# Expert rows of u and v stored side by side and gathered as pairs of 8 KB in the last stage of a two-block transformer kernel

## The chip, the cores and the metric

One NeuronCore of a Trainium2 chip runs the whole program. The metric is the device time in microseconds of one execution, lower is better. TensorE multiplies into PSUM, VectorE and ScalarE work elementwise and reduce, GpSimd issues most of the small and all of the indexed transfers here, SyncE issues the weight loads; 16 DMA engines carry all transfers.

## The reference

Two transformer blocks on 512 tokens of width 1024 in float32. The second block ends with a layer of retrieved experts (`_peer`), and the change is in that layer alone:

```python
def _peer(h, wq, k1, k2, u_tab, v_tab):
    ...
        q = (t @ wq).reshape(PEER_BLOCK, PEER_HEADS, 2, PEER_DQ // 2)
        ...
        v1, i1 = lax.top_k(s1, PEER_TOPK)
        v2, i2 = lax.top_k(s2, PEER_TOPK)
        cand = (v1[..., :, None] + v2[..., None, :]).reshape(...)
        score, ci = lax.top_k(cand, PEER_TOPK)
        expert = (... i1 ... * PEER_NKEYS + ... i2 ...)
        g = jax.nn.softmax(score, axis=-1).astype(t.dtype)
        act = jax.nn.gelu(jnp.einsum('thkd,td->thk', u_tab[expert], t))
        return jnp.einsum('thk,thkd->td', g * act, v_tab[expert]).astype(t.dtype)
```

Each token picks 8 heads x 16 = 128 of 16384 experts. For each it needs a row of u (1024 floats, 4 KB) for a dot product with the token, and the row of v with the same index for a weighted sum. That is 512 x 128 x 2 rows of 4 KB, 537 MB.

## The kernel before

Tokens lie in four tiles of 128, one token to a partition. One gather (`gather`, L2753) fetches for choice j of tile i the rows of all 128 tokens: 128 rows of 4 KB, 512 KB. There are 4 x 128 for u and as many for v, 1024 rows of work in the words of the kernel.

- `FETCH` is the order of gathers and of work: u rows, and behind them v rows, 16 of them within the 128 u rows of tile 0, then five v rows to four u rows, so that the v rows catch up with the u rows at the end.
- `PLACES` are buffers of 4 KB a partition: 7 until row 144, then 19. A gather waits until the row that had its place before was used: a dot for u, an add for v (`PREV`). All gathers stand on GpSimd's queue in the order of `FETCH`.
- For a u row VectorE makes the dot product (L2783). After every 16 of them (`BL`) it works out the polynomial of the gelu (L2788 to L2790), ScalarE the sigmoid (L2716), VectorE the weights (L2791, L2793).
- For a v row ScalarE makes a diagonal matrix of the weights (L2722, four buffers `DG`), and TensorE adds diagonal x row into PSUM (L2706, two matmuls of 512 columns, four records in the trace). An add is called by its row.
- The experts are chosen by `select_tensor` (scores, L2568), `select_scalar` (L2587 copies the scores, L2593 exponentiates) and `select_vector` (L2612 to L2663). One choice is that of one head in one tile: 32 in all. `EXU[i]` holds the indices.
- `in_order` weaves this on every engine: after each row of work the function `advance` lets the choices go on by two steps until row 128, then by two and one in turn, and the tail of the layer before (among it the queries of tiles 1 to 3, L258) by one step in three turns. If a gather needs indices that aren't there yet, `advance` runs until they are.
- At the end of a tile (v row 127) VectorE, ScalarE and GpSimd normalize and write the tile (L2806 to L2816, L2725, `to_power` at L263). `XHR` holds the rest of the sum; `LATE` are rows of constants.

## Time and profile before

| | us |
|---|---|
| median of 3 runs | 4134.59 |
| lowest, highest | 4134.58, 4135.83 |
| profiled execution | 4141.38 |
| its span, first to last instruction | 4139.6 |

Mean granted TensorE clock 0.936 of full speed. Busy shares of the span: TensorE 83%, VectorE 51%, ScalarE 22%, GpSimd 34%. The layer of experts with what is woven into it runs from 2463 us to the end. In the rows below PE is TensorE, PEld its weight load, DVE VectorE, ACT ScalarE, POOL GpSimd; a row of a timeline gives start, duration, engine, line, operation, count, and in brackets the idle time before it with what ended it.

### The profile page before, as it was taken

How to read it: one execution, taken by the hardware profiler on the slowest of the kernel's cores; microseconds unless marked ns; L12 is line 12 of the kernel's file. 1: busy time of each engine (PE TensorE's matmuls, PEld its weight loads, DVE VectorE, ACT ScalarE, POOL GpSimd, SP SyncE). 2: the span in 40 equal slices, each digit the busy share in tenths (PEclk: the TensorE clock that was granted, in tenths of full speed). 3: DMA queues.
4: the chain of work that ended last, by engine and by line, in shares of the span. 5: the costliest groups of instructions: out<-in, count | busy, mean ns of one | idle time of the engine just before them, and what ended most of it. 6: DMA issues, size and time to landing. Idle time of an engine off the chain costs nothing.

```text
span 4139.6 us, 32033 instructions
## 1 busy us (share of the span) xinstructions
PE 3437.5 (83%) x10366; PEld 1709.8 (41%) x10366; DVE 2123.9 (51%) x4564; ACT 906.0 (22%) x1862; POOL 1419.8 (34%) x1337
## 2 busy tenths in 40 slices
PE   8468998999998889988899974669776777788787
PEld 4344544444454454534444564234332323232222
DVE  0567424422004366757425449864686877444443
ACT  1224412000014123632211323111221222111111
POOL 0214410000000004700001013443777777777775
PEclk9768999999999999999999987789999899999999
DMA  3010021433221122211212356765999999999997
GB/s 143 21 51 1 1 102 51 162 134 151 102 82 41 66 87 69 93 67 56 92 61 81 130 189 216 260 233 189 350 380 356 332 378 376 380 409 409 367 408 314
DMA packets 171908, 764.63 MB, mean 185 GB/s; under 512 B 19256, under 2 KB 19256, under 8 KB 160224
## 3 DMA queue, kind: packets, MB, share of 16 engines
q0 software_dynamic: 157904, 580.06, 37.4%
q1 hardware_dynamic: 13824, 182.51, 12.0%
q8 instruction: 85, 1.39, 0.1%
q14 instruction: 79, 0.65, 0.0%
q10 hardware_dynamic: 16, 0.02, 0.0%
HBM read 743.62 MB, written 18.89 MB: 184 GB/s over the span
## 4 chain that ended last, share of the span: by engine, by line
PE 47%; DVE 16%; DMA 9%; POOL 9%; issue 6%; ACT 3%; POOLq 0%; DVEq 0%; ACTq 0%
PE ps L252 14%; PE ps L258 12%; POOL arena L2753 9%; DMA arena<-in_pu,arena 7%; DVE arena L2783 5%; PE ps L1346 5%; PE ps L1416 5%; DMA arena<-in_pv,arena 2%; PE ps L2706 2%; PE ps L220 2%; PE ps L1722 1%; PE ps L1710 1%; PE ps L2331 1%; PE ps L786 1%; PE ps L1031 1%
## 5 line engine op out<-in xcount | busy, mean ns | idle before, releaser
L2706 PE MATMUL ps<-arena 128*128 128x512 f32 x2048 | 999.4, 628 | 333.1 <-DMA arena<-in_pv,arena 169.5
L2783 DVE CUSTOM_DVE_ANT_0 arena<-arena 128x1024 f32<-128x1024 f32 x512 | 623.5, 1221 | 385.9 <-DMA arena<-in_pu,arena 385.2
L252 PE MATMUL ps<-arena 128*128 128x512 f32 (+1 forms) x1768 | 760.8, 591 | 31.2 <-ACT arena L2272 24.4
L2706 PEld LDWEIGHTS ps<-arena 128*128 128x128 f32 x2048 | 375.4, 196 | 936.1 <-issue 499.8
L2753 POOL DMA_INDIRECT arena<-in_pu,arena x512 | 546.1, 1067 | 373.2 <-DVE arena L2659 76.9
L2753 POOL DMA_INDIRECT arena<-in_pv,arena x512 | 548.4, 1071 | 196.1 <-issue 109.1
L258 PE MATMUL ps<-arena 128*128 128x512 f32 (+2 forms) x1408 | 532.4, 539 | 3.1 <-DVE arena L1263 0.9
L252 PEld LDWEIGHTS ps<-arena 128*128 128x128 f32 x1768 | 339.4, 193 | 438.5 <-issue 433.3
L258 PEld LDWEIGHTS ps<-arena 128*128 128x128 f32 x1408 | 268.8, 192 | 264.0 <-issue 218.6
L220 PE MATMUL ps<-arena 128*128 128x128 f32 x1046 | 192.9, 320 | 200.9 <-ACT arena L812 49.6
L2722 ACT ACTIVATE arena<-arena 128x128 f32<-128x128 f32 x512 | 191.6, 396 | 565.6 <-PE ps L2706 519.4
L1416 PE MATMUL ps<-arena 128*128 128x512 f32 x640 | 291.8, 607 | 24.7 <-ACT arena L1801 17.4
L263 POOL TENSOR_TENSOR arena<-arena 128x1 f32<-128x1 f32 (+7 forms) x38 | 61.3, 1615 | 687.7 <-DVE arena L630 291.8
L220 PEld LDWEIGHTS ps<-arena 128*128 128x128 f32 x1046 | 140.4, 162 | 286.4 <-issue 144.1
L1440 POOL DMA_DIRECT2D aside<-arena x20 | 10.7, 534 | 622.4 <-ACT arena L1430 622.4
L1346 PE MATMUL ps<-arena 128*128 128x512 f32 x512 | 221.5, 593 | 1.4 <-DVE arena L1380 1.4
L1416 PEld LDWEIGHTS ps<-arena 128*128 128x128 f32 x640 | 120.6, 195 | 161.5 <-issue 143.2
L1072 POOL TENSOR_SCALAR arena<-arena 128x128 f32<-128x128 f32 (+3 forms) x96 | 111.3, 1171 | 155.9 <-DVE arena L1103 87.7
L1246 POOL DMA_DIRECT2D x_spill<-arena x1 | 0.6, 573 | 464.3 <-DVE arena L1377 464.3
L1346 PEld LDWEIGHTS ps<-arena 128*128 128x128 f32 x512 | 96.7, 190 | 125.7 <-issue 123.4
L1554 DVE SCALAR_TENSOR_TENSOR ps<-arena,ps 128x512 f32<-128x512 f32 x150 | 113.4, 756 | 5.2
L1574 POOL TENSOR_TENSOR arena<-arena 128x512 f32<-128x512 f32 x90 | 105.4, 1171 | 24.3 <-ACT arena L1517 12.0
(342 smaller groups left out, 3218.1 us busy)
## 6 DMA issues: line engine op xcount, KB each, us to landing
arena<-in_w_in SPq DMA_DIRECT2D x27, 2048.0 KB, 9.0
arena<-in_w_ada SPq DMA_DIRECT2D x12, 2048.0 KB, 8.2
arena<-in_w_ff_in SPq DMA_DIRECT2D x8, 2048.0 KB, 12.7
arena<-in_w_ff_out SPq DMA_DIRECT2D x8, 2048.0 KB, 12.7
...
```

Source lines behind the costliest of these rows:

```text
L220: return t.transpose(ps, src, ID[0:src.shape[0], 0:src.shape[0]])
L252: x = t.matmul(PS[:, b, 0:n], hT[:, k, i * 128:(i + 1) * 128], w[:, k, :], start=k == 0, stop=k == nk - 1)
L258: x = t.matmul(PS[:, b, 0:n], w[:, k, f * 128:(f + 1) * 128], hT[:, k, 0:n], start=k == 0, stop=k == nk - 1)
L1072: g.tensor_scalar(probs(i, h), probs(i, h), r[:, 6 + h:7 + h], None, ALU.mult).then_inc(*at1.G.step("scaled", i, h))
L1346: x = t.matmul(PS[:, 4 * c + i, :], AT[:, 8 * kk + k, 128 * i:128 * i + 128], w[:, k, :], start=kk == 0 and k == 0, stop=kk == 3 and k == 7)
L1416: x = t.matmul(PS[:, b, :], l, r, start=k == 0, stop=k == 7)
L1554: tap.V.own(v).scalar_tensor_tensor(out=sums, in0=u[:, j:j + 512], scalar=tap_weight(k, j), in1=sums, op0=ALU.mult, op1=ALU.add).then_inc( ...
L1574: tap.G.own(g).tensor_tensor(cv, cv, TAPP[(30 * n + j - 1) % 3], ALU.add).then_inc(*tap.G.step("sum", 30 * n + j - 1))
L2706: x = t.matmul(PS[:, b + c, :], DG[n % 4], row(f)[:, 512 * c:512 * c + 512], start=j == 0, stop=j == 127)
L2722: a.activation(DG[n % 4], ID, ACT.Copy, scale=GS[i][:, j:j + 1]).then_inc(*pe.A.step("dg", n))
L2753: g.indirect_dma_start(PLACES[SPOT[n]], None, d[tab], bass.IndirectOffsetOnAxis(ap=EXU[i][:, j:j + 1], axis=0)).then_inc(s_row_in[SPOT[n]] ...
L2783: v.tensor_tensor_reduce(row(f), row(f), TT[i], 1.0, 0.0, ALU.mult, ALU.add, DOT[i % 2][:, j:j + 1]).then_inc(*pe.V.step("dot", 128 * i + j))
```

## The change

- The tables u and v are stored as one table `uv` of rows of 8 KB, u then v of the same expert (built with the weights on the host).
- Tile 0 works as before, with 7 places of 4 KB (`CELLS`) and rows of 4 KB: it reads `uv` as a table of half rows with twice the index, and `EXV` is the index of the v half. Its first 16 v rows stand where they stood; the other 112 now follow all u rows of the tile, ahead of tile 1.
- Tiles 1 to 3 gather u and v row together: 384 gathers of 128 x 8 KB, 1 MiB each, into 14 places (`PAIRS`), each held from the gather to the add. The v row of a choice is worked `LAG` = 6 choices behind its u row. Six of the places are the panels used before, eight are other pieces; some overlap the places of tile 0 (`SHARED`).
- In tiles 1 to 3 the gelu is worked in blocks of 4 instead of 16, and its polynomial takes two operations instead of three in all tiles.
- Some loads and operations of the end of a tile stand at other v rows (24 to 80, 96 to 112, 100 to 116), and `YY` and `XHR` lie elsewhere.

```diff
-        BL = 16
-        FETCH = []
+        BLOCK = (16, 4, 4, 4)
+        LAG = 6
+        UV = d["uv"]
+        HALVES = UV.rearrange("e (s n) -> (e s) n", s=2)
...
+        WORK = []
         done_v = 0
-        for n_ in range(1, 513):
-            FETCH.append(("pu", (n_ - 1) // 128, (n_ - 1) % 128))
-            goal = 0 if n_ < 64 else (n_ - 64) // 4 if n_ < 128 else 16 + (n_ - 128) * 5 // 4 if n_ < 512 else 512
...
+        for n_ in range(1, 129):
...
+            while done_v < (n_ - 64) // 4:
+                WORK.append(("pv", 0, done_v))
                 done_v += 1
-        ROWS = len(FETCH)
-        PLACES = [piece(o_cs + 1024), piece(o_ka + 1024), piece(o_ka + 2048), piece(o_cs), MIXf[:, 0:1024], piece(o_ht + 1024), piece(o_ka)]
-        FEW = len(PLACES)
-        PLACES += [panel("w_pq+", c)[:, 1024 * j:1024 * j + 1024] for c in (1, 2, 3) for j in range(4)]
-        MANY = len(PLACES)
-        FROM = 144
-        SPOT = [n % FEW if n < FROM else (n - FROM) % MANY for n in range(ROWS)]
...
+        WORK += [("pv", 0, j_) for j_ in range(done_v, 128)]
+        for n_ in range(384 + LAG):
+            if n_ < 384:
+                WORK.append(("pu", 1 + n_ // 128, n_ % 128))
+            if n_ >= LAG:
+                WORK.append(("pv", 1 + (n_ - LAG) // 128, (n_ - LAG) % 128))
...
+        CELLS = [piece(o_cs + 1024), piece(o_ka + 1024), piece(o_ka + 2048), piece(o_cs), MIXf[:, 0:1024], piece(o_ht + 1024), piece(o_ka)]
+        FEW = len(CELLS)
+        PAIRS = [panel("w_pq+", c)[:, 2048 * j:2048 * j + 2048] for c in (1, 2, 3) for j in range(2)]
+        PAIRS += [piece(o, 2048) for o in (o_va + 1024, o_ka + 2048, o_qa + 2048, o_ka, o_cs, W0, o_t + 2048, o_ht)]
+        MANY = len(PAIRS)
+        SHARED = {7: (2,), 9: (6, 1), 10: (3, 0), 11: (4,), 13: (5,)}
+        FETCH = [f for f in WORK if f[1] == 0]
+        SPOT = [n % FEW for n in range(256)]
+        FETCH += [("uv",) + f[1:] for f in WORK if f[1] and f[0] == "pu"]
+        SPOT += [FEW + n % MANY for n in range(384)]
...
+        for n_ in range(FETCHES):
+            k_ = SPOT[n_]
+            PREV.append([held_by[k_]] if uses[k_] else [held_by[c] for c in SHARED.get(k_ - FEW, ())])
+            uses[k_] += 1
+            NTH.append(uses[k_])
+            held_by[k_] = FETCH[n_]
...
+        def emptied(f):
+            return ("pu" if f[0] == "pu" else "pv",) + f[1:]
+        FREED = [max((WHEN[emptied(f)] for f in before), default=-1) for before in PREV]
...
         def row(f):
-            return PLACES[SPOT[NUMBER[f]]]
+            n = number(f)
+            if f[1] == 0:
+                return CELLS[SPOT[n]]
+            o = 1024 * (f[0] == "pv")
+            return PAIRS[SPOT[n] - FEW][:, o:o + 1024]
...
+        EXV = piece(o_ht + 2432, 128).bitcast(U32)
...
+                    if i == 0:
+                        pe.V.own(v).tensor_scalar(EXV[:, hs], EXU[0][:, hs], 1, None, ALU.add).then_inc(*pe.V.step("selv", h))
...
-                while n < ROWS and PREV[n] < r:
+                while n < FETCHES and FREED[n] < r:
...
-                yield FETCH[r]
+                yield WORK[r]
...
+                    bl = BLOCK[i]
+                    if tab == "pu" and j % bl == bl - 1:
+                        a.wait_ge(*pe.V.at("poly", i, j // bl))
+                        a.activation(T3[:, 0:bl], T3[:, 0:bl], ACT.Sigmoid, scale=2.0 * 0.7978845608028654
+                                     ).then_inc(*pe.A.step("gelu", i, j // bl))
...
+                if i == 0:
+                    g.wait_ge(*(pe.V.at("sel", 0, j // 16) if tab == "pu" else pe.V.at("selv", j // 16)))
+                    x = (EXU[0] if tab == "pu" else EXV)[:, j:j + 1]
+                    g.indirect_dma_start(CELLS[k], None, HALVES, bass.IndirectOffsetOnAxis(ap=x, axis=0)).then_inc(s_row_in[k], 16)
+                else:
+                    g.wait_ge(*pe.V.at("sel", i, j // 16))
+                    g.indirect_dma_start(PAIRS[k - FEW], None, UV, bass.IndirectOffsetOnAxis(ap=EXU[i][:, j:j + 1], axis=0)
+                                         ).then_inc(s_row_in[k], 16)
...
-                if f == ("pv", 0, 24):
+                if f == ("pv", 0, 80):
...
+                    bl = BLOCK[i]
+                    if j % bl == bl - 1:
+                        c = slice(j - bl + 1, j + 1)
+                        x, w, y = DOT[i % 2][:, c], GS[i][:, c], T3[:, 0:bl]
+                        pe.V.own(v).scalar_tensor_tensor(out=y, in0=x, scalar=0.044715, in1=x, op0=ALU.mult, op1=ALU.mult
+                                                         ).then_inc(*pe.V.step())
+                        pe.V.own(v).scalar_tensor_tensor(out=y, in0=y, scalar=1.0, in1=x, op0=ALU.add, op1=ALU.mult
+                                                         ).then_inc(*pe.V.step("poly", i, j // bl))
                         v.tensor_tensor(w, w, x, ALU.mult).then_inc(*pe.V.step())
-                        v.wait_ge(*pe.A.at("gelu", i, j // BL))
-                        pe.V.own(v).tensor_tensor(w, w, y, ALU.mult).then_inc(*pe.V.step("wg", i, j // BL))
```

What follows is the order of instructions in the two programs.

TensorE, tile 0, from the scores in the middle of it: L258 are the queries of tiles 1 to 3 (`x8` is one chunk), L2706 the adds of v rows, two to an add. Before:

```order
L2568 MATMUL ps<-arena 128x128 x4
L2706 MATMUL ps<-arena 128x512 x2
L258 MATMUL ps<-arena 128x384 x16
L2706 MATMUL ps<-arena 128x512 x2
L258 MATMUL ps<-arena 128x384 x40
L2706 MATMUL ps<-arena 128x512 x4
```

The same place now (L2597 is L2568, L2740 is L2706):

```order
L2597 MATMUL ps<-arena 128x128 x4
L2740 MATMUL ps<-arena 128x512 x2
L258 MATMUL ps<-arena 128x384 x16
L2740 MATMUL ps<-arena 128x512 x2
L258 MATMUL ps<-arena 128x384 x8
L2740 MATMUL ps<-arena 128x512 x2
L258 MATMUL ps<-arena 128x384 x8
L2740 MATMUL ps<-arena 128x512 x6
```

The five chunks that stood in one piece, and the five behind them with an add or two between, now have three adds between them, all of tile 0.

GpSimd, from the v rows of tile 0 to the first pairs of tile 1. Now (before, u and v gathers take turns here):

```order
L2800 DMA arena<-in_uv,arena 128x1024 x16
L2814 DMA arena<-in_rows 128x1024 x5
L2815 DMA arena<-ada_rows 128x1024
L2800 DMA arena<-in_uv,arena 128x1024 x41
L2803 DMA arena<-in_uv,arena 128x2048 x10
L263 TENSOR_TENSOR arena<-arena 128x1
```

Ten pairs are issued before GpSimd's part of the end of tile 0 (L263).

VectorE, tile 1, choices between dots (L2783 is a dot with its accumulator read). Before:

```order
L2783 ISA arena<-arena 128x1024
L2783 ISA arena 128x1
L2616 MATCH_REPLACE arena<-arena 128x128
L2618 MAX arena<-arena 128x8
L2620 MAX_INDEX arena<-arena 128x8
L2783 ISA arena<-arena 128x1024
L2783 ISA arena 128x1
L2612 MAX arena<-arena 128x8
```

The same kind of place now (L2833 is the dot, L2641 to L2697 are L2612 to L2663):

```order
L2833 ISA arena<-arena 128x1024
L2833 ISA arena 128x1
L2839 SCALAR_TENSOR_TENSOR arena<-arena 128x4
L2841 SCALAR_TENSOR_TENSOR arena<-arena 128x4
L2843 TENSOR_TENSOR arena<-arena 128x4
L2845 TENSOR_TENSOR arena<-arena 128x4
L2666 CAST arena<-arena 128x32
L2669 TENSOR_TENSOR arena<-arena 128x256
L2641 MAX arena<-arena 128x8
L2643 MAX_INDEX arena<-arena 128x8
```

Every fourth dot has the four operations of a gelu block behind it, and there are on average three steps of a choice between two dots. Of the choices, six are now done beside the v rows of tile 0, where no dots stand, and 17 beside the 161 dots behind them.

## Rows read from the trace of the kernel before

**Rows 1.** The page: GB/s in 40 slices of 103.5 us, and the packets.

```profile
GB/s 143 21 51 1 1 102 51 162 134 151 102 82 41 66 87 69 93 67 56 92 61 81 130 189 216 260 233 189 350 380 356 332 378 376 380 409 409 367 408 314
DMA packets 171908, 764.63 MB, mean 185 GB/s; under 512 B 19256, under 2 KB 19256, under 8 KB 160224
```

**Rows 2.** Windows of the expert stage: length, busy time by engine, clock, DMA share, GB/s.

```profile
core 0: us, PE busy (x) PEld busy (x) DVE busy (x) ACT busy (x) POOL busy (x), PEclk, DMA share, GB/s
2860.00:2880.00 20.00, 17.12 (x49) 8.59 (x48) 11.25 (x33) 2.86 (x8) 11.69 (x12) 1.00 0.72 253
3100.00:3500.00 400.00, 297.36 (x659) 120.60 (x658) 316.42 (x888) 81.29 (x210) 313.14 (x274) 0.94 0.97 360
3600.00:3700.00 100.00, 82.32 (x173) 29.97 (x173) 44.78 (x80) 16.83 (x45) 76.54 (x79) 1.00 1.03 409
```

**Rows 3.** A window at the program's start, while weights arrive in rows of 16 KB.

```profile
6.00:28.00 22.00, 13.44 (x48) 9.56 (x49) 5.91 (x9) 6.00 (x10) 1.02 (x1) 1.00 1.02 430
```

**Rows 4.** Timeline of GpSimd: gathers, among them number 600 and number 1000.

```profile
3104.35 1.96 POOL L2753 DMA_INDIRECT arena<-in_pv,arena  x1 [0.31 <-DVE arena L2614]
...
3551.51 0.94 POOL L2753 DMA_INDIRECT arena<-in_pu,arena  x1 [0.30 <-issue]
...
4079.74 1.00 POOL L2753 DMA_INDIRECT arena<-in_pv,arena  x1 [0.30 <-issue]
```

**Rows 5.** Timeline of TensorE in tile 0: scores, adds, and chunks of L258.

```profile
2816.03 1.13 PE L2568 MATMUL ps<-arena 128*128 128x128 f32 x8 [0.67 <-ACT arena L2378]
...
2833.24 1.96 PE L2706 MATMUL ps<-arena 128*128 128x512 f32 x4 [0.96 <-ACT arena L2722]
...
2883.42 5.34 PE L258 MATMUL ps<-arena 128*128 128x384 f32 x16
2889.72 3.67 PE L2706 MATMUL ps<-arena 128*128 128x512 f32 x8 [0.96 <-ACT arena L2722]
```

**Rows 6.** Timeline of the last tile's end: 18 adds, then VectorE's first and last operation.

```profile
4095.34 31.15 PE L2706 MATMUL ps<-arena 128*128 128x512 f32 x72 [1.82 <-ACT arena L2722]
...
4126.52 1.22 DVE L2806 TENSOR_TENSOR arena<-ps,arena 128x1024 f32<-128x1024 f32 x1 [31.41 <-PE ps L2706]
...
4134.69 1.23 DVE L2816 TENSOR_TENSOR arena<-arena 128x1024 f32<-128x1024 f32 x1
```

**Rows 7.** Timeline of VectorE: first and nearly last operation of one choice.

```profile
2452.83 0.30 DVE L2612 MAX8 arena<-arena 128x8 f32<-128x128 f32 x1 [1.17 <-ACT arena L2587]
...
2463.38 0.23 DVE L2659 TENSOR_SCALAR arena<-arena 128x16 f32<-128x16 f32 x1
```

**Rows 8.** Timeline of VectorE: a dot between two operations of a choice.

```profile
3213.14 0.42 DVE L2620 FIND_INDEX8 arena<-arena 128x8 uint32<-128x256 f32 x1
3213.48 1.21 DVE L2783 CUSTOM_DVE_ANT_0 arena<-arena 128x1024 f32<-128x1024 f32 x1
3214.61 0.08 DVE L2783 DVE_READ_ACCUMULATOR2_ANT arena<- 128x1 f32 x1
3214.73 0.17 DVE L2646 TENSOR_SCALAR arena<-arena 128x16 uint32<-128x16 uint32 x1
```

**Rows 9.** Timeline of VectorE: first and last operation of a gelu block.

```profile
4094.06 0.17 DVE L2788 TENSOR_TENSOR arena<-arena 128x16 f32<-128x16 f32 x1
...
4094.93 0.18 DVE L2793 TENSOR_TENSOR arena<-arena 128x16 f32<-128x16 f32 x1 [0.20 <-ACT arena L2716]
```

**Rows 10.** Groups of VectorE from 3220 to 3500 us that waited for ScalarE.

```profile
L2612 DVE MAX8 arena<-arena 128x8 f32<-128x128 f32 (+1 forms) x33 | 11.2, 341 | 12.3 <-ACT arena L2587 10.9
...
L2662 DVE RECIPROCAL arena<-arena 128x1 f32<-128x1 f32 x12 | 2.0, 164 | 3.4 <-ACT arena L2593 3.0
```

**Rows 11.** ScalarE's table load in a timeline, and one row of the DMA issues.

```profile
3135.71 1.28 ACT L2716 ACT_TABLE_LOAD   x1
...
arena<-in_ctx POOLq DMA_DIRECT2D x1, 1024.0 KB, 5.3
```

**Rows 12.** Timeline of TensorE: an add behind a gap.

```profile
2680.24 3.75 PE L2706 MATMUL ps<-arena 128*128 128x512 f32 x4 [5.04 <-ACT arena L2722]
```

88 lines of the change are left out of this document (44 added, 44 removed).

## The prediction

> **What bounds the kernel now.** I read the slices of the page first, then windows, then the timelines of GpSimd, TensorE and VectorE in the expert stage, which runs from 2463 us to the end. [rows 1] is the page's line of GB/s: from slice 29 on (about 2900 us) the core moves 350 to 410 GB/s, nowhere else as much. [rows 2] splits this. From 3600 to 3700 us the DMA engines are full (share 1.03, 409 GB/s), and GpSimd issues 79 gathers in 100 us; with the 0.30 us that stand before each of them, it is full too. From 3100 to 3500 us the rate is 360 GB/s: 274 gathers with 313.1 us of GpSimd plus 274 x 0.30 = 82 us, together 395 of 400. So there GpSimd's issue is the bound, as some gathers take 1.96 us instead of 0.94 [rows 4] while VectorE chooses experts. Around 2860 us neither is full (253 GB/s in that window, [rows 2]): TensorE works on the queries, in chunks of L258 [rows 5]. The chain of waits agrees: gathers, landings and dots take turns in it.
>
> Counting the gathers along GpSimd's timeline, number 144 (the first of tile 1) starts at 2836 us, number 600 at 3551.5 and number 1000 at 4079.7 [rows 4]: 1.32 us a row in the last part, two thirds of a tile end included, 2.64 us for a u and a v row.
>
> **Up to 2835 us nothing moves.** The TensorE order is the same up to the 15th add of tile 0, which starts at 2833.2 us [rows 5]. The smaller gelu of this stretch is unchanged (blocks of 16), its polynomial one operation of about 0.2 us shorter, and eight small operations for the v index are added: zero, under TensorE's work.
>
> **The middle: v rows of tile 0 alone.** In the new order the last 10 chunks of L258 stand with 26 adds of tile 0 (one chunk and 1 add, eight times a chunk and 3 adds, one chunk and 1 add), and the u rows of tile 1 that went beside them come later. A chunk is 5.34 us, the wait before the next add 0.96, two adds 3.67, a third 1.73 [rows 5, 6]: 8 x 11.5 + 2 x 8.1 = 108 us, to about 2943. 41 adds are then done. The other 87 have nothing beside them but three groups of scores (1.13 us and about 0.9 of waits each, [rows 5]): 87 x 1.73 (18 adds in 31.15 us, [rows 6]) = 150.5, + 6, + 2 for the late rows: TensorE ends tile 0 at 3102. Seven places are enough for that: a place comes round every 7 x 1.73 = 12 us, and a small gather lands in 5 to 6. The DMA engines run at 136 to 305 GB/s meanwhile; this is the loss of the change. Its cover is that 14 pairs are fetched from about 3090 on. Then VectorE ends the tile, 9.4 us from L2806 to L2816 [rows 6]; GpSimd gets to its part of it after ten pairs, 10 x 1.25 from 3090, just in time. The first dot on a pair starts at 3112.
>
> **The choice phase: VectorE becomes the bound.** Choices advance with the rows, three steps to two rows, before and after; so 17.3 heads are chosen beside the 161 dots that follow (before, one in 8.2 dots; now one in 9.3), and VectorE has for each: 161 dots x 1.17 (a dot pushes its neighbours 1.17 us apart, 3213.56 to 3214.73, [rows 8]) = 188; 17.3 heads x 11.2 (10.8 from the first MAX8 to L2659's end, the rest behind it, [rows 7]) = 194; 40 gelu blocks of four operations x 0.84 (a block of five operations takes 1.05, [rows 9]) = 34; the end of tile 1, 9.4 + 2; XHR 2.5. That is 430 us. Waits on ScalarE come on top: 10.9 + 3.0 us for 11 heads in 280 us now [rows 10], so 22; table loads of 1.28 us [rows 11] are twice as many, mostly done while ScalarE waits for VectorE anyway: 4, bounds 0 and 40. In all 456 us, 2.83 a pair: the DMA engines (2.48, below) and GpSimd (1.3 to 2.3 a pair) have slack. The phase ends at 3568.
>
> **The rest: DMA.** About eight pairs are then fetched ahead, 215 are not. What does a pair of 8 KB rows cost? The trace has no gathers of that size. From below: the weight loads of 16 KB rows at the start move 430 GB/s [rows 3], 2.44 us for 1 MiB. From above: twice a 4 KB gather at 409 GB/s, 2.56. I take a fixed part and a part by size through the two points: 160 ns for 4 KB and 610 for 16 KB on one engine give 310 for 8 KB, so 2.48 us a pair. 215 x 2.48 = 533; landing of the first 5.3 [rows 11]; the end of tile 2 keeps VectorE 12 us from dots, of which the 14 places cover all but 3. Last landing 3568 + 541 = 4109. The Trainium skill (DMA: Bandwidth & Descriptors, Why small descriptors are slow) gives a packet a fixed cost of about 3 cycles beside one for each 32 B; by that 8 KB rows would win 1.1% over 4 KB rows, an estimate of 2.53 us a pair and 11 us more in the sum. The two rows above differ by 5%, so I leave the sum as it is.
>
> **The tail.** ScalarE reaches the scale of v row j-6 behind the gelu of u row j, so with blocks of 4 seven adds, not four, come after the last dot: 1.3 + 0.4 + 0.25 + 0.5 to the first add, 7 x 1.73 + 0.2: 14.8. Now 18 adds and 32.5 us stand there [rows 6], but most of them beside the last v gathers. From TensorE's end to the end of the span 13.1, as now (4126.5 to 4139.6).
>
> **Sum.** 4109.5 + 14.8 + 13.1 = 4137.4, against the span of 4139.6: minus 2 us. The profiled execution is 6.8 us above the median of the runs, which I take as common to both: 4134.6 - 2 = **4132 us**. A gain of 33 us in the last part (215 pairs x 0.16) is eaten by the middle, where 112 rows go at TensorE's pace.
>
> **Rivals.**
> - *Faster: the waits of the choice phase vanish.* TensorE and ScalarE no longer wait for landings, six rows behind, so scores may be ready when VectorE asks: minus 22. With pairs at 430 GB/s another 215 x 0.04 = 9. Time 4101 to 4112. For it: nearly all of the 10.9 us come from adds that wait for landings. Against it: ScalarE is tied to VectorE at each block of four.
> - *Slower: TensorE is late for the scores.* With blocks of four it gets its adds in bursts of 7 us and then waits 4. After such a gap an add takes 3.75 us instead of 1.96 [rows 12]: the half clock, 1.2 GHz. Nine score groups then come 2 adds x 1.8 = 3.6 later, 32 in all, less the 6 that VectorE has to spare: plus 26, 4158. It decides from the point where the four adds of a block and the score group no longer end within the 11.4 us of four pairs. Where the granted clock stays near 1, it costs nothing.
> - *Slower: 8 KB rows are no faster by the byte than 4 KB rows.* 215 x 0.08 = 17: 4149; with the smaller win of 1%, 4143. For it: the start was loaded from another queue. The rule of the skill above speaks for this one.
> - *The change does not do what it says:* the descriptors of a row of 8 KB are made in two, GpSimd pays twice and stays at 2.86 us a pair: plus 60. Of 171908 packets 11684 are of 8 KB or more [rows 1], more than the some 10500 that the weight loads of 16 KB rows make (82 x 128), so GpSimd's direct loads of 8 KB rows are among them in one piece; this is unlikely.
>
> **How the numbers follow.** Forecast 0.42 (its own range 4120 to 4146, from the bounds of the middle, +-8, and of the table loads); waits vanish 0.25; late scores 0.17; no gain by row size 0.13; two descriptors 0.03. A measurement of this kernel tells 0.2%, 8.3 us, from no change: below 4126.3 is faster, above 4142.9 slower. Of the forecast 0.12 lie below, 0.24 between, 0.06 above; of the first rival 0.23 and 0.02; of the no-gain one 0.03 between and 0.10 above; the others above. Faster 0.35, same 0.29, slower 0.36. The range from 4104 to 4158 leaves out the far parts of the first two rivals and the last.
>
> **What would show it.** The last add of tile 0 near 3100 us, and about 300 GB/s or less from 2940 to 3090; VectorE over 90% busy from 3112 to near 3568, at 350 to 370 GB/s; behind that 420 to 425 GB/s with VectorE near 55%; a gather of a pair 1 to 2 us long on GpSimd; seven adds after the last dot. Wrong would be: tile 0 done before 3080 (the middle isn't TensorE's), VectorE with idle time in the choice phase (waits on ScalarE, or late pairs), or a rate in the last part of 409 or 430.

## The result and the profile after

| | before | after |
|---|---|---|
| median, us | 4134.59 | 4158.41 |
| lowest, highest (5 runs each) | 4132.02, 4139.55 | 4155.26, 4158.82 |
| profiled execution | 4141.38 | 4158.82 |
| its span | 4139.6 | 4157.0 |

The ratio of the times is 1.0061, with a 95% interval of 1.0049 to 1.0073: the change makes the kernel slower by 0.6%. Three later pairs of measurements gave 1.0058, 1.0067 and 1.0048. The predicted time was 4132 and its range 4104 to 4158, so the median lies 26 us above the one and 0.4 above the other.

The page's slices and packets of the changed kernel, the counterpart of [rows 1]:

```profile
GB/s 143 20 51 1 1 102 54 159 142 141 101 81 41 66 86 76 86 66 61 97 50 99 115 202 216 259 245 190 240 322 390 384 372 325 400 421 410 418 421 302
DMA packets 116610, 764.59 MB, mean 184 GB/s; under 512 B 13112, under 2 KB 13112, under 8 KB 55776
```

The packets fell from 171908 to 116610, as 384 gathers of 128 rows are in packets of 8 KB. Slice 28 (from 2910 us) moves 240 GB/s, and the slices behind 3600 us reach 421. The windows, to be held against [rows 2] (length; busy time of the engines; clock; DMA share; GB/s):

```profile
2860.00:2880.00 20.00, 18.08 (x48) 8.73 (x47) 10.24 (x40) 4.31 (x11) 5.68 (x6) 1.00 0.38 114
2950.00:3100.00 150.00, 143.04 (x341) 63.81 (x340) 50.00 (x177) 33.49 (x92) 82.59 (x89) 0.99 0.86 306
3100.00:3500.00 400.00, 285.05 (x588) 119.67 (x586) 336.90 (x995) 96.00 (x235) 158.39 (x143) 0.85 0.95 376
3600.00:3700.00 100.00, 78.94 (x156) 32.17 (x155) 54.03 (x119) 13.79 (x50) 44.51 (x40) 0.90 1.01 421
```

At 2860 us the rate has fallen from 253 GB/s to 114, from 3100 to 3500 it rose from 360 to 376, and from 3600 on from 409 to 421. GpSimd, which was full, now has 158 of 400 us and 45 of 100. So two stretches gained and one lost. How much, a count of the gathers says. It gives the rows of 4 KB that GpSimd had not yet asked for (a pair is two):

| at, us | before: rows left | after: rows left |
|---|---|---|
| 2835 | 880 | 879 |
| 2946 | 839 | 848 |
| 3116.6 | 718 | 742 |
| 3498 | 458 | 482 |
| 3570.9 | 408 | 434 |
| 4000 | 85 | 90 |
| last gather starts | 4108.9 | 4113.6 |
| end of the span | 4139.6 | 4157.0 |

In the middle, while tile 0 ends alone, the changed kernel falls 24 rows behind. In the choice phase it holds that distance and no more (two gained or lost). In the last part it makes good most of it: 434 rows in 542.7 us, 1.25 us each, where the kernel before needed 538 for 408, 1.32 each. The last gather is 4.7 us later; the other 12.7 of the 17.4 us come behind it, where a pair's landing and seven adds take the place of the last v rows' landings.

In the kernel before, GpSimd had no slack in the last part. Its waits ahead of its gathers from 3600 to 3700 us (total, times, longest) are all of 0.3 us or less, so it never stood waiting for a place:

```profile
POOL arena L2753 <- issue: 14.3, 47, 0.3
POOL arena L2753 <- PE ps L2706: 8.5, 28, 0.3
```

The 409 GB/s there are therefore as much the pace of GpSimd's issue as that of the DMA engines.

The end of tile 0 on VectorE and the first dots on pairs (start, duration, operation, wait in brackets):

```profile
3106.81 1.23 DVE L2858 TENSOR_TENSOR arena<-ps,arena 128x1024 f32<-128x1024 f32 x1 [12.37 <-PE ps L2740]
...
3114.99 1.23 DVE L2868 TENSOR_TENSOR arena<-arena 128x1024 f32<-128x1024 f32 x1
...
3116.59 1.22 DVE L2833 CUSTOM_DVE_ANT_0 arena<-arena 128x1024 f32<-128x1024 f32 x1
```

What VectorE waited for from there to dot number 160 (counted from 0), 3116 to 3571 us:

```profile
DVE arena L2641 <- ACT arena L2616: 19.1, 6, 4.0
DVE arena L2845 <- ACT arena L2751: 11.1, 39, 3.5
DVE arena L2696 <- ACT arena L2622: 6.4, 11, 1.2
DVE arena L2858 <- PE ps L2740: 2.7, 1, 2.7
```

Not one of them is a landing. Dot 160, the last choice's index and, from dot 168 on, the first dots that wait for a landing:

```profile
3570.87 1.22 DVE L2833 CUSTOM_DVE_ANT_0 arena<-arena 128x1024 f32<-128x1024 f32 x1
3572.01 0.08 DVE L2833 DVE_READ_ACCUMULATOR2_ANT arena<- 128x1 f32 x1
3572.12 0.18 DVE L2687 SCALAR_TENSOR_TENSOR arena<-arena 128x16 uint32<-128x16 f32 x1
...
3583.54 1.23 DVE L2833 CUSTOM_DVE_ANT_0 arena<-arena 128x1024 f32<-128x1024 f32 x1 [0.49 <-DMA arena<-in_uv,arena]
...
3587.57 1.23 DVE L2833 CUSTOM_DVE_ANT_0 arena<-arena 128x1024 f32<-128x1024 f32 x1 [2.79 <-DMA arena<-in_uv,arena]
```

The last dot and the end of the last tile, the counterpart of [rows 6]:

```profile
4128.87 1.23 DVE L2833 CUSTOM_DVE_ANT_0 arena<-arena 128x1024 f32<-128x1024 f32 x1 [1.19 <-DMA arena<-in_uv,arena]
...
4144.16 1.23 DVE L2858 TENSOR_TENSOR arena<-ps,arena 128x1024 f32<-128x1024 f32 x1 [13.22 <-PE ps L2740]
```

### The profile page after: what moved, and what is told of

Read it like the earlier page. It is cut to its first block, busy times and chain, and to the rows that moved or that the text cites. A ratio compares the mean times of both kernels' runs of the same rounds, so it can differ in the third digit from the quotient of the medians.

```text
span 4157.0 us, 31690 instructions
## 1 busy us (share of the span) xinstructions
PE 3463.3 (83%) x10366; PEld 1753.1 (42%) x10366; DVE 2152.1 (52%) x4828; ACT 910.3 (22%) x1946; POOL 1025.2 (25%) x953
## 2 busy tenths in 40 slices
DMA packets 116610, 764.59 MB, mean 184 GB/s; under 512 B 13112, under 2 KB 13112, under 8 KB 55776
## 4 chain that ended last, share of the span: by engine, by line
PE 51%; DVE 20%; DMA 10%; issue 4%; ACT 3%; POOL 2%; DVEq 0%; POOLq 0%; ACTq 0%
PE ps L252 14%; PE ps L258 12%; DMA arena<-in_uv,arena 10%; DVE arena L2833 7%; PE ps L2740 6%; PE ps L1346 5%; PE ps L1416 5%; PE ps L220 2%; POOL arena L2803 1%; PE ps L1722 1%; DVE arena L2643 1%; PE ps L1031 1%; DVE arena L2649 1%; DVE arena L2645 1%; PE ps L786 1%
## 5 line engine op out<-in xcount | busy, mean ns | idle before, releaser
L2740 PE MATMUL ps<-arena 128*128 128x512 f32 x2048 | 1020.0, 655 | 330.2 <-ACT arena L2758 307.2
L2740 PEld LDWEIGHTS ps<-arena 128*128 128x128 f32 x2048 | 416.0, 209 | 913.3 <-issue 855.9
L2833 DVE CUSTOM_DVE_ANT_0 arena<-arena 128x1024 f32<-128x1024 f32 x512 | 622.9, 1219 | 240.3 <-DMA arena<-in_uv,arena 240.1
L2803 POOL DMA_INDIRECT arena<-in_uv,arena x384 | 435.6, 1134 | 563.9 <-PE ps L2740 350.0
L258 PE MATMUL ps<-arena 128*128 128x512 f32 (+2 forms) x1408 | 532.3, 538 | 3.1 <-DVE arena L1263 0.9
L252 PEld LDWEIGHTS ps<-arena 128*128 128x128 f32 x1768 | 339.3, 193 | 437.6 <-issue 432.5
L258 PEld LDWEIGHTS ps<-arena 128*128 128x128 f32 x1408 | 268.3, 191 | 263.8 <-issue 219.5
L2800 POOL DMA_INDIRECT arena<-in_uv,arena x256 | 265.1, 1035 | 385.4 <-PE ps L2740 144.7
L1416 PE MATMUL ps<-arena 128*128 128x512 f32 x640 | 291.6, 606 | 24.7 <-ACT arena L1801 17.4
L220 PEld LDWEIGHTS ps<-arena 128*128 128x128 f32 x1046 | 141.0, 162 | 284.6 <-issue 146.6
L263 POOL TENSOR_TENSOR arena<-arena 128x1 f32<-128x1 f32 (+7 forms) x38 | 61.2, 1613 | 715.8 <-DVE arena L630 291.5
L1346 PE MATMUL ps<-arena 128*128 128x512 f32 x512 | 221.5, 593 | 1.4 <-DVE arena L1380 1.4
L2758 ACT ACTIVATE arena<-arena 128x128 f32<-128x128 f32 x512 | 173.1, 389 | 123.7 <-PE ps L2740 110.2
L2751 ACT ACTIVATE arena<-arena 128x4 f32<-128x4 f32 (+1 forms) x104 | 21.5, 207 | 806.5 <-DVE arena L2841 806.4
L1416 PEld LDWEIGHTS ps<-arena 128*128 128x128 f32 x640 | 120.5, 195 | 161.4 <-issue 143.1
L1346 PEld LDWEIGHTS ps<-arena 128*128 128x128 f32 x512 | 96.7, 190 | 125.7 <-issue 123.4
## 6 DMA issues: line engine op xcount, KB each, us to landing
arena<-in_w_ff_out SPq DMA_DIRECT2D x8, 2048.0 KB, 12.7
```

Source lines behind the costliest of these rows:

```text
L220: return t.transpose(ps, src, ID[0:src.shape[0], 0:src.shape[0]])
L252: x = t.matmul(PS[:, b, 0:n], hT[:, k, i * 128:(i + 1) * 128], w[:, k, :], start=k == 0, stop=k == nk - 1)
L258: x = t.matmul(PS[:, b, 0:n], w[:, k, f * 128:(f + 1) * 128], hT[:, k, 0:n], start=k == 0, stop=k == nk - 1)
L1346: x = t.matmul(PS[:, 4 * c + i, :], AT[:, 8 * kk + k, 128 * i:128 * i + 128], w[:, k, :], start=kk == 0 and k == 0, stop=kk == 3 and k == 7)
L1416: x = t.matmul(PS[:, b, :], l, r, start=k == 0, stop=k == 7)
L2740: x = t.matmul(PS[:, b + c, :], DG[n % 4], row(f)[:, 512 * c:512 * c + 512], start=j == 0, stop=j == 127)
```

## The experiments

The times are medians; "changed" is the changed kernel. It was measured four times, each beside a kernel before of 4130 to 4135 on the same chip: 4158.4, 4154.9, 4158.8 and 4155.6 us. On two further occasions the kernel before took 4219 and 4231 us, and there the changed kernel did not run; where a version ran on one of those the text says so, and its distance from the changed kernel is then one between occasions. From the traces (all in us of the span; dots on pairs are counted from 0):

| kernel | first dot | dot 160 | last dot | span | median |
|---|---|---|---|---|---|
| changed | 3116.6 | 3570.9 | 4128.9 | 4157.0 | 4158.4 |
| slower choices | 3114.7 | 3516.2 | 4080.2 | 4107.6 | 4110.5 |
| two gathers a pair | 3129.2 | 3605.8 | 4198.0 | 4227.1 | 4226.7 |
| distance 4 | 3115.5 | 3568.7 | 4120.3 | 4144.3 | 4147.6 |
| distance 8 | 3111.8 | 3560.1 | 4123.4 | 4154.2 | 4156.9 |
| gelu blocks of 2 | 3116.7 | 3604.5 | 4162.7 | 4190.1 | 4191.8 |
| mixed middle | 2954.4 | 3531.1 | 4087.6 | 4115.0 | 4115.7 |
| slower choices, distance 4 | 3117.7 | 3517.7 | 4080.2 | 4104.1 | 4105.7 |
| these and mixed | 2948.9 | 3495.5 | 4057.0 | 4080.9 | 4083.1 |
| these, tile ends apart | 2947.6 | 3488.3 | 4049.4 | 4073.3 | 4075.4 |
| these, a fifth place | 2951.2 | 3484.6 | 4046.6 | 4070.6 | 4072.6 |

### Slower choices

```diff
-                drain(chosen, 2 if r < 128 or turns[0] % 2 else 1)
+                drain(chosen, 1 if r >= 256 else 2 if r < 128 or turns[0] % 2 else 1)
```

> The changed kernel with one edit: from row 256 of the order on (the first pair), a choice advances one step a row (two a pair) instead of three steps to two rows. No work is left out. Theory A, VectorE bounds the choice phase: VectorE's work for a pair falls to 1.17 (dot) + 0.21 (a quarter of a gelu block) + 2 steps x 0.40 (11.2 us for 28 steps of a choice) = 2.2 us, with the waits on ScalarE 2.35, under the 2.49 that a pair takes in the DMA-bound part. The pairs then go at 2.49 to 2.52 us from the first dot at 3116 on: last dot 3116 + 383 x 2.51 = 4077, median about 4107, 52 us below the changed kernel and 27 below the kernel before. VectorE is never over 95% busy behind 3116, the last choice ends near 3750. Theory B, the choice phase is slow because TensorE gets its adds in bursts at half clock and frees places late: bursts are the same, the phase goes on at 2.8 a pair and lasts until the last choice: 4160 to 4190.

It took 4110.49 us (4106.45 to 4111.99), beside a kernel before of 4231. The window from the first dot to 3700 us, and VectorE's waits in it:

```profile
3115.00:3700.00 585.00, 446.18 (x968) 186.72 (x969) 489.96 (x1379) 133.91 (x365) 260.84 (x230) 0.92 1.00 415
```

```profile
DVE arena L2833 <- DMA arena<-in_uv,arena: 35.7, 74, 2.5
DVE arena L2641 <- ACT arena L2616: 15.6, 7, 3.4
DVE arena L2845 <- ACT arena L2751: 12.0, 57, 0.9
```

The dots now wait for landings already while experts are chosen, and the DMA engines' share is 1.00. The 160 pairs from the first dot took 401.5 us, 2.51 each, where the changed kernel took 2.84. Theory A's 4107 is met within 4 us; theory B, which had the phase go on at 2.8, is refuted. The last choice now ends at 3713 us instead of 3572. The same bytes and the same VectorE work in another proportion are worth some 48 us.

### Two gathers a pair

Each pair comes in two gathers of 4 KB rows, from tables of u and of v; who waits for a pair waits for both.

```diff
-                    g.indirect_dma_start(PAIRS[k - FEW], None, UV, bass.IndirectOffsetOnAxis(ap=EXU[i][:, j:j + 1], axis=0)
-                                         ).then_inc(s_row_in[k], 16)
+                    for half, tab_ in enumerate(("pu", "pv")):
+                        g.indirect_dma_start(PAIRS[k - FEW][:, 1024 * half:1024 * half + 1024], None, d[tab_],
+                                             bass.IndirectOffsetOnAxis(ap=EXU[i][:, j:j + 1], axis=0)).then_inc(s_row_in[k], 16)
```

> The changed kernel with one edit: each pair is fetched by two gathers of 4 KB rows, u and v, into the same place, from two tables of their own; order, places, gelu blocks as changed. It measures what 8 KB rows are worth by themselves. If a 4 KB gather takes 1.28 us of the DMA engines (409 GB/s) and a pair 2.487 (422 GB/s), the 222 pairs behind 3571 us take 2.56 each: plus 16 us, 4174. If the row size is worth nothing: 4158. If GpSimd's issue comes in (two gathers of 0.94 to 1.96 us and 0.30 before each, 2.5 to 4.5 a pair, 2.9 as in the kernel before while VectorE chooses): the 161 pairs of the choice phase take 2.9 instead of 2.83 as well, plus 11: 4185.

4274.35 us (4269.45 to 4282.26), on the occasion on which the kernel before took 4231. As that left the size open, it ran once more beside the changed kernel.

> The kernel with two 4 KB gathers a pair once more, beside the changed kernel and the kernel before on one chip. On the chip of the first call it took 4274 us, at 365 to 375 GB/s behind 3600 us with the DMA engines' share at 0.97 to 0.99, but the kernel before took 4231 there, 97 more than elsewhere, and has as many 4 KB gathers. If that chip (or where its tables lay) was slow with 4 KB gathers alone: here 409 GB/s behind 3600 us, 2.56 a pair, and 4170 to 4180. If a pair in two gathers is slow everywhere (GpSimd's issue with 0.30 before each): 4260 to 4275 here too, with the kernel before at 4134.

Here it took 4226.68 us (4209.82 to 4228.98) beside 4158.82 for the changed kernel and 4129.71 for the one before: 68 us above the changed kernel. So no expectation held: row size alone was priced at 4174, with GpSimd's issue at 4185. The traces part the 70.1 us between the spans: the first dot is 12.6 later, the 160 pairs behind it take 22.3 more, the rest 34.2 more, the tail 1. In the choice phase (3150 to 3450 us) and behind it (3620 to 3720):

```profile
3150.00:3450.00 300.00, 215.07 (x459) 90.84 (x458) 249.11 (x756) 70.81 (x180) 239.05 (x202) 0.90 0.95 348
3620.00:3720.00 100.00, 73.72 (x151) 30.02 (x149) 51.31 (x114) 12.77 (x47) 77.49 (x75) 0.91 1.01 392
```

and GpSimd's gathers in the first of these windows (count, busy us, mean ns, idle before them):

```profile
L2804 POOL DMA_INDIRECT arena<-in_pv,arena x100 | 123.3, 1233 | 30.5 <-issue 23.5 <-DVE arena L2846 1.2 <-DVE arena L2649 1.2
L2804 POOL DMA_INDIRECT arena<-in_pu,arena x101 | 116.3, 1152 | 34.7 <-issue 18.0 <-PE ps L2740 5.4 <-DVE arena L2645 1.5
```

239.6 us of gathers and 65 before them are the whole of 300: GpSimd is the bound at 348 GB/s, as it was in the kernel before. From 3620 to 3720 us it is full as well, 77.5 us and 0.3 before each of 74 gathers, and none of them waited longer:

```profile
POOL arena L2804 <- issue: 19.8, 65, 0.3
POOL arena L2804 <- PE ps L2740: 1.8, 6, 0.3
```

The 56.5 us of both parts go with the number of issues. What the row size does to the DMA engines by itself this run does not tell, as they were not the only bound in either window; a DMA share of 1.01 at 392 GB/s, and of 1.01 at 421 with pairs, says that the share doesn't either. Why the first dot is 12.6 us later was not followed up. Put together, by the medians taken side by side: order, places, distance and gelu blocks of the change cost 97 us (4129.7 to 4226.7), and the pair gathers give 68 back.

### The distance from dot to add

```diff
-        LAG = 6
+        LAG = 4
```

> The changed kernel with one edit: the add of a pair's v row stands 4 rows behind its dot, not 6. A place then comes free two pairs earlier, so two more of the 14 are in flight or landed. Theory A (at the end of the choice phase there was no stock of landed pairs because 6 to 9 of the 14 places wait for their add): the stock at the hand-over is 2 pairs larger, minus 5 us; the adds behind the last dot are five, not seven, minus 3.5: 4150. If the missing stock has another cause: 4155, by the tail alone. If the shorter distance lets TensorE or ScalarE hold up VectorE (ScalarE is tied to it at each block of four): above 4158.

4147.63 us (4146.10 to 4158.67), on the occasion on which the kernel before took 4231. And with `LAG = 8`:

> The changed kernel with one edit: the add of a pair stands 8 rows behind its dot, not 6. Theory A (places are held until their add, and that is why no stock of landed pairs stood at the end of the choice phase): 8 to 11 of the 14 places wait for their add, 3 to 6 are in flight, and a landing takes 13.7 us, so also the choice phase waits for landings and the DMA engines idle in the last part: at 4.5 pairs in flight per some 12.5 us 2.8 us a pair, 222 x 0.3 = 67 us more at worst, at the least 5 for the stock and 3.5 for the two more adds at the end: 4170 to 4225, 4190 as the middle. Rival, places don't matter: 4162.

4156.92 us (4155.48 to 4167.21), beside 4154.94 for the changed kernel. The expected 4190 was wrong. What VectorE waited for from 3570 to 3620 us with 4, and with 8:

```profile
DVE arena L2833 <- DMA arena<-in_uv,arena: 15.7, 15, 1.3
```

```profile
DVE arena L2833 <- DMA arena<-in_uv,arena: 21.4, 21, 1.3
```

In the last part all three move 421 GB/s. In the steady state 9, 7 and 5 pairs were issued and not yet dotted with distances of 4, 6 and 8. One of them has landed, so with 8 some four are in flight (3.9 on average from 3620 to 3720 us, 3 to 5), and these are enough to keep the DMA engines full: a pair then just spends less time in the queue, as the times from issue to landing show (minimum, median, maximum; with 8 for all 384 pair gathers, with 4 for the 54 whose landing the trace has; it was 13.7 in the median with 6):

```profile
DMA to landing us min/median/max: 5.5/10.1/20.8
```

```profile
DMA to landing us min/median/max: 5.7/18.0/23.8
```

What the distance does move is the stock at the end of the choice phase, the pairs that have landed and are not yet dotted. The first dot that waits for a landing behind dot 160 is number 170 with a distance of 4, 168 with 6, 165 with 8, and the 20 pairs from dot 160 on take 1.94, 2.20 and 2.35 us each. Against 2.487 that is a stock of 4.4, 2.3 and 1.1 pairs. The landings themselves, counted at the start of dot 160, give three pairs ahead with a distance of 6 and one with 8. The tail from the last dot to the end is 24.0, 28.1 and 30.8 us. Both together are the 7 to 11 us that the distance of 4 gains; with 8 the part from dot 160 to the last dot is 5.3 us longer and the tail 2.7, but in the profiled execution its first dot was 4.8 us earlier and its choice phase 6.0 shorter (448.3 us), so no loss is left. Why, was not followed up.

### Gelu blocks of two

```diff
-        BLOCK = (16, 4, 4, 4)
+        BLOCK = (16, 2, 2, 2)
```

> The changed kernel with gelu blocks of 2 instead of 4 for tiles 1 to 3. VectorE then has 80 blocks of 0.84 instead of 40 in the choice phase, ScalarE twice the sigmoids, TensorE bursts of two adds with half the gap. Theory A (the choice phase is VectorE's work): plus 40 x 0.84 = 34 in 161 pairs, 3.04 a pair, nothing behind it as VectorE has slack there, and one or two adds less at the end: 4185. Theory B (bursts of adds at the half clock make scores late and frees places late): the waits of 27 us on ScalarE's copies and exponentials shrink to 10, and the end of the block's add comes earlier: 4158 + 34 - 17 = 4175 if the blocks cost VectorE in full, less if their waits are hidden; a time under 4160 would say that bursts cost more than I think.

4191.84 us (4188.15 to 4197.27), on the occasion on which the kernel before took 4219. VectorE's waits from 3110 to 3600 us:

```profile
DVE arena L2845 <- ACT arena L2751: 22.7, 79, 3.5
DVE arena L2641 <- ACT arena L2616: 13.9, 5, 5.0
DVE arena L2696 <- ACT arena L2622: 8.4, 11, 1.2
```

First dot to dot 160: 487.8 us against 454.3, so 33.5 more, where theory A had 34. VectorE was busy 22.2 us longer (413.0 against 390.8), and the waits for sigmoids grew by 11.6. The waits for scores and exponentials (L2641, L2696) are 22.3 us, hardly less than the 25.5 of the changed kernel, although the adds come in twos. So their size does not hang on the size of the bursts, as theory B had it, and every operation on VectorE, with its waits for sigmoids, counts in this phase in full. What the half clock by itself costs there this run does not tell: with gaps between the adds still there, the granted clock from 3100 to 3600 us was 0.89.

### The mixed middle

From v row 44 of tile 0 on, one pair of tile 1 stands beside each v row. The places are dealt out anew for it, the four diagonals go round by the order of the adds, and the load of `XHR` for tile 1 moves from v row 64 to 104.

```diff
+        ALONE = 44
...
-        WORK += [("pv", 0, j_) for j_ in range(done_v, 128)]
+        WORK += [("pv", 0, j_) for j_ in range(done_v, ALONE)]
+        done_v = ALONE
         for n_ in range(384 + LAG):
+            if done_v < 128:
+                WORK.append(("pv", 0, done_v))
+                done_v += 1
```

> The changed kernel with one edit of the order: from v row 44 of tile 0 on, each v row stands with a pair of tile 1 (with the places that this needs). Distance 6, pace of the choices and tile ends as in the changed kernel. Slower choices with the distance of 4, and the same with mixing and split ends, gave 4105.7 and 4072.6 on one chip: mixing beside slow choices is worth some 25. Theory (the stretch of tile-0 v rows alone wastes DMA time and VectorE time both): 84 steps of 4.0 from 2950 bring the order to 3286 with 84 dots done and 13 of the 21 open heads chosen beside them; 8 heads are left for 75 pairs at 2.83, then 225 pairs at 2.51: last dot 3286 + 212 + 565 = 4063, median 4093, 65 below the changed kernel and 40 below the kernel before: the way the middle is ordered then is what made the change slower. Rival: the stretch alone costs only its idle DMA share (25% of 156 us) less what mixing wastes (8): minus 30, 4127, the same as before.

4115.74 us (4112.99 to 4116.85), on the occasion on which the kernel before took 4219. That is 39 to 43 below the changed kernel, between the two expectations. The windows of the stretch and of the end of tile 0:

```profile
2950.00:3050.00 100.00, 84.00 (x191) 34.89 (x189) 73.26 (x223) 26.94 (x65) 55.58 (x56) 0.97 1.01 411
3250.00:3300.00 50.00, 34.18 (x85) 15.43 (x84) 36.05 (x106) 14.01 (x33) 19.88 (x19) 0.89 0.69 264
```

411 GB/s instead of 306: the stretch is now the DMA engines'. Dot 80 stood at 3271.8, as expected (84 at 3286). The miss lies behind it: I had priced the next 75 pairs at 2.83 and forgotten that the ends of tiles 0 and 1 fall among them; pairs 80 to 100 took 3.81 and 120 to 140 took 3.54 us each. At dot 160 the gain is 39.8 us, and it is 41.3 at the last dot. So the stretch of v rows alone costs some 40 us. That is more than the 24 us of median by which the whole change is slower, and under half of the 97 that order, places, distance and blocks cost together. Without it the change would have been a gain: 4115.7, against 4130 to 4135 on the other occasions. That it would take the same time there was not measured; the pair of kernels below that was measured side by side has 33 us for mixing and the tile ends together.

### Both remedies together

Slower choices and a distance of 4, first without the mixed middle:

> The changed kernel with the slower choices (one step a row from row 256) and the distance of 4 from dot to add together, for what mixing is worth beside them. Slower choices gave 4110.5 and the distance of 4 gave 4147.6, against 4155 to 4158 for the changed kernel. In the version with slower choices there is no choice phase bound by VectorE, so the two more pairs in flight no longer buy a stock at a hand-over; what is left of the distance are two adds less at the end, 3.5, and cover at the tile ends, 0 to 10: 4100 to 4107, 4104. If they add up in full: 4102. Against the mixed version's 4083 that leaves some 20 us for mixing; if this kernel comes out at 4085 or less, mixing is worth nothing.

4105.74 us (4100.92 to 4111.79), ratio to the kernel before 0.9941 (0.9924 to 0.9958): as expected, the stock is worth nothing where no VectorE phase ends. With the mixed middle:

> A version that removes the stretch of tile-0 v rows alone: from v row 44 of tile 0 on, each v row of tile 0 stands with one pair of tile 1 (11 of the 14 pair places and four of the small ones are used meanwhile), the distance from dot to add is 4, and choices advance one step a row from row 256 on. All work is done. Theory: the middle ran at TensorE's pace with the DMA engines at 291 to 316 GB/s, and that is the loss of the change. From about 2950 on 84 v rows and 84 pairs then take 1.25 + 2.49 = 3.74 us together, 314 us, to 3265; the other 300 pairs 2.49 each, to 4012; tail and end 13 + 13: a span of 4038, median 4040, minus 118. Rival: TensorE at half clock (2 adds of 1.75 each in 3.74 us, with waits between) becomes the bound of the mixed stretch, 4.2 a step: plus 40, 4080. Rival: the mixed order has too few pairs in flight (places are held by the distance of 4 and blocks of 4), 4.5 a step: 4105.

4083.13 us (4080.26 to 4083.59), beside a kernel before of 4231. The expected 4040 was 43 too low: the first 80 steps of the mixed stretch took 317 us, 3.97 each and not 3.74, which is 18; the 303 pairs behind them took 2.61 us each and not 2.52, most of it at the ends of tiles 0 and 1 (dots 80 to 100 took 3.56 us each, 120 to 140 3.04). The end of tile 0 (a window, and what GpSimd waited for):

```profile
3250.00:3300.00 50.00, 34.01 (x79) 15.19 (x79) 29.77 (x75) 10.94 (x27) 21.90 (x20) 0.83 0.70 278
```

```profile
POOL arena L263 <- DVE arena L2885: 17.0, 1, 17.0
```

GpSimd's power function for the tile's variance stood ahead of its gathers. It was then put 12 rows, and VectorE's last three operations 20 rows, behind the last add:

```diff
+        END_G = {min(WHEN[("pv", i, 127)] + 12, ROWS - 1): i for i in range(4)}
+        END_V = {min(WHEN[("pv", i, 127)] + 20, ROWS - 1): i for i in range(4)}
...
-                if f and f[0] == "pv" and f[2] == 127:
-                    g.wait_ge(*pe.V.at("var", f[1]))
+                at_ += bool(f)
+                if at_ in END_G and f:
+                    g.wait_ge(*pe.V.at("var", END_G[at_]))
...
```

> The mixed version with the end of each tile taken apart: GpSimd's power function stands 12 rows and VectorE's last three operations 20 rows behind the last add of the tile, so that neither waits for the other. All work is done. In the mixed version the window 3250 to 3300 moved 278 GB/s, as GpSimd waited 17 us for VectorE's variance: 0.3 x 50 = 15 us of DMA time, and at the ends of tiles 1 and 2 about 8 us each (388 and 393 GB/s in windows of 100 us, against 421). Theory: nearly all of the 31 us come back, 4083 - 28 = 4055. Rival: the gathers held back there only meet places that TensorE frees late, or the last tile's end is what counts: 4075 to 4083.

4075.36 us (4071.18 to 4078.63), ratio 0.9871 (0.9836 to 0.9907). The same window now:

```profile
3250.00:3300.00 50.00, 37.89 (x87) 16.75 (x86) 32.32 (x86) 12.64 (x34) 25.43 (x22) 0.89 0.84 341
```

Eight us, not 28: dots 80 to 100 took 6.8 us less, so the end of tile 0 came back in part, and there was nothing to gain at the next two (dots 120 to 160 took 106.4 us before and 107.2 now, 260 to 300 took 101.6 and 102.0). The last version takes a fifth small place, and has one pair place less for it:

```diff
-        KEPT, BOTH = (0, 1, 3, 6), [p for p in range(MANY) if not set(SHARED.get(p, ())) & set((0, 1, 3, 6))]
+        KEPT, BOTH = (0, 1, 2, 3, 6), [p for p in range(MANY) if not set(SHARED.get(p, ())) & set((0, 1, 2, 3, 6))]
```

> The mixed version with the tile ends taken apart, with five small places and 11 pair places in the mixed stretch instead of four and 12 (12 and 11 by the list of shared places: pair place 7 waits). There a pair and a v row took 3.9 to 4.25 us instead of the 3.77 that their bytes need (2.49 + 1.28), as v rows wait for a place behind adds that wait for a gelu block. With a fifth place 84 steps at 3.8: minus 12, 4063. If places don't matter there, and the gelu blocks hold up ScalarE, unchanged at 4075; with a pair place less it could lose 5.

4072.60 us (4072.48 to 4076.49), ratio 0.9863 (0.9847 to 0.9880). The exchange is worth nothing that can be told. This is the fastest version: 57 us below the kernel before and 33 below the version with slower choices and the distance of 4, both measured beside it.

### The kernel before on other occasions

> The changed kernel itself, unedited, on this chip. The last call's runs stood beside a kernel before of 4231 us, where the first measurement had 4135; if that difference is between chips, the changed kernel is needed beside them. If the chip is slower at everything: 4158 x 1.023 = 4255. If it is slower only where GpSimd issues gathers of 4 KB rows (the kernel before has 1024 of them, the changed one 256 beside 384 of pairs): within 15 us of 4158.

4154.94 us (4152.78 to 4160.15), beside 4134.0 for the kernel before: this occasion was not a slow one.

> The kernel before, unedited, for its trace on this chip. If its slower time comes from GpSimd's gathers: the mean gather in the last part is over 1.0 us (0.94 in the first trace), GpSimd is busy or issuing all the time and the DMA engines move under 400 GB/s there; up to 2463 us, where no gather is issued, the two traces agree within 3 us. If the DMA engines or HBM are slower: as many gathers stand waiting for places as before, and the share of the DMA engines stays above 1.

4137.03 us in one run, and 409 GB/s from 3620 to 3720 us.

> The changed kernel, unedited, as the control of this call. 4152 to 4160 as on two chips so far. Should the kernel before be near 4231 again, the changed kernel stays at 4155 if slowness there belongs to 4 KB gathers.

4158.82 us (4155.36 to 4161.70), beside 4129.71.

> The kernel before for its trace. In two of four calls it took 4219 and 4231 us, in two 4130 and 4134. If this chip is one of the first sort: gathers of 4 KB rows take longer behind 3500 us, at 360 to 380 GB/s with the DMA engines' share still near 1, as the kernel with two gathers a pair showed on such a chip (365 to 375 GB/s, and 394 to 409 on the other sort), and nothing differs up to 2463 us. If it is of the second sort: 4130 to 4137, 409 GB/s there.

4129.94 us in one run, again with 409 GB/s.

> The changed kernel beside it. On a chip where the kernel before takes 4220 or more the changed kernel has not run yet. If only gathers of 4 KB rows are slow there, its 256 of them (at TensorE's pace, under 316 GB/s) hide it: 4155 to 4165, and the change is then a gain of 1.5%. If rows of 8 KB are slow there too: 4200 and over; the related kernels that ran there (4110 with slower choices, 4148 with the distance of 4, 4116 mixed) speak against that.

4155.55 us (4154.72 to 4158.40), beside 4134.87. None of these met an occasion on which the kernel before takes over 4200. It need not be a matter of the chip: the one with 4219 and the one with 4134.87, five minutes later, have the same chip number on record. So why the kernel before took 4219 and 4231 stays open, and with it whether the change would be a gain there. What there is: the kernel with two gathers a pair took 4274 there and 4227 here, and its rate in a window of the last part was lower. There, and here, 3600 to 3700 us:

```profile
3600.00:3700.00 100.00, 71.85 (x145) 29.94 (x146) 52.08 (x122) 16.50 (x53) 75.33 (x70) 0.89 0.97 365
```

```profile
3600.00:3700.00 100.00, 74.57 (x147) 30.20 (x146) 55.35 (x128) 16.27 (x53) 77.75 (x74) 0.88 0.99 378
```

The versions with pairs that ran there moved 421 GB/s in the last part, as here. What differs in the traces of the two executions lies on GpSimd's queue, which is the bound of this kernel: from 3600 to 3900 us it issued 210 gathers there and 222 here, their mean was 1.07 us against 1.03, and 13 us of its waits there the profile puts down to no engine of this core. A kernel with pairs has slack on this queue. That this is why pairs don't show it is an inference, and what slowed the queue was not seen.

## Why the prediction was right or wrong

In span time the prediction was 4137.4, and the changed kernel took 4157.0: 19.6 us more. By its steps:

1. **Nothing moves up to 2835 us**: right. The 15th add starts at 2833.62, and as many rows are left at 2835.
2. **The middle is TensorE's and ends at 3102**: right in kind, 4.7 us short. TensorE is busy 143 of the 150 us from 2950 to 3100; the last add is done at 3106.8. The chunks of L258 end as forecast, add 41 is done at 2944.1 us; the other 87 took 4.2 us more. Their one long wait is 4.7 us ahead of 3032, an add that waits for a landing, while the late rows of constants are loaded. I had put 2 us there:

```profile
PE ps L2740 <- DMA arena<-in_uv,arena: 4.7, 1, 4.7
PE ps L2740 <- ACT arena L2758: 2.3, 2, 1.1
```

3. **Tile end and first dot at 3112**: 9.4 us for the end as said, the dot at 3116.6.
4. **The choice phase is VectorE's, 456 us**: right in the bound and, with some luck, in the size, 454.3 us. The waits for scores and exponentials, set at 22, were 25.5; those for sigmoids 11.1. All waits were 44 us where the sum has some 36 (22, 4, and about 10 inside the terms of gelu blocks and tile end), and the operations with the small gaps between them 410 where it has 420. So VectorE was busy for 390.8 of 454.3 us, 86% and not over 90%, which the prediction had named as a sign:

```profile
3116.60:3570.90 454.30, 328.51 (x679) 138.49 (x680) 390.79 (x1177) 109.41 (x273) 177.30 (x157) 0.86 0.93 369
```

The experiment with slower choices shows the bound by taking it away, that with blocks of two by adding 33.5 us to it.
5. **The rate in the last part, 2.48 us a pair**: right. 421 GB/s and dots 2.49 us apart. The working is weaker than its result: one of its two points, 409 GB/s with 4 KB rows, is also the pace at which GpSimd issued, as its waits above show, so it need not be what the DMA engines do with such rows. The rule of the Trainium skill (DMA: Bandwidth & Descriptors, Why small descriptors are slow), with its estimate of 2.53 us, is a gain of 1% over 4 KB rows. [rows 2] and the window above have 409 and 421, 3%, but for the same reason they neither confirm the rule nor refute it.
6. **"About eight pairs are then fetched ahead, 215 are not"**: this is the step that failed. When dot 160 started, at 3570.87 us, 167 pairs had been issued, but issued is not fetched: 164 had landed, that of dot 160 among them (161, 162 and 163 at 3565.3, 3567.8 and 3570.3 us; 164 came at 3572.8). Three pairs were ahead, not eight, and 220 were still to land. The three later traces of the changed kernel have 164, 164 and 163. From dot 160 to the last dot the prediction had 541.5 us (533 for 215 pairs, 5.3, 3), and it took 558.0:

- five more pairs at 2.487 us: 12.4;
- 0.007 us a pair of pace: 1.5;
- two loads of `XHR` and the writing of tile 2, 512 KB each, which have no term in the sum: 3.7 at 421 GB/s;
- what is left is 7.2 us in which the DMA engines were not full, against the 8.3 set: -1.1. It lies behind dot 160, at the end of tile 2 and at the last pairs.

```profile
3571.00:3621.00 50.00, 44.94 (x93) 18.61 (x92) 31.20 (x70) 9.98 (x31) 25.52 (x23) 0.90 1.00 410
3821.00:3871.00 50.00, 37.86 (x78) 15.56 (x77) 32.87 (x66) 9.06 (x28) 21.71 (x21) 0.86 0.96 391
```

In the choice phase the pairs came at the pace of VectorE because places came free at that pace: GpSimd waited 148.6 us for adds, and a released place became a request only then. Of the 14 places seven held pairs that were dotted and not yet added, and the other seven were issued, three of them still on their way.

```profile
POOL arena L2803 <- PE ps L2740: 148.6, 68, 7.8
POOL arena L2803 <- DVE arena L2833: 27.7, 19, 5.9
```

7. **The tail, 27.9 us**: right, 28.1.

So 4.6 us came from the middle, minus 1.7 from the choice phase, 16.5 from the last part, 0.2 from the tail: 19.6. A last share is in the way from the span to the median. The prediction carried the 6.8 us by which the profiled execution of the kernel before lay above its median over to the changed kernel, whose own lay 0.4 above: 6.4 us of the miss of 26.4. The sum was best made against the profiled execution and the median left as a separate uncertainty.

**The rivals.** *The waits vanish*: no, they were 25.5 us. *TensorE is late for the scores*: it gave the time (4158) and not the cause. The adds do come at half clock behind gaps (mean clock 0.85 from 3100 to 3500), but with adds in twos the waits for scores and exponentials stayed, and they exceed the 22 us of the forecast by 3.5, not by 26. *8 KB rows are no faster by the byte*: its price is refuted, as a pair took 2.487 us and not 2.56; what 4 KB rows would do with a queue that has slack was not measured. *Two descriptors a row*: no; GpSimd has slack, and there are fewer packets. What no rival covered is that the last part of the kernel before may have been GpSimd's; the prediction saw it full there too and went on with the DMA engines alone. That changes no term of the sum, but it says where the gain of that part comes from. The range of 4104 to 4158 fell short on its upper side because nothing in it stood for the stock. Its bound was easy to name: no pair ahead at all, 8 x 2.48 = 20 us.
